# VectorE makes the first low part between the scalings of the second half, in the stage changes that have a shift

## The reference

```python
def modulate(h, shift, scale):
    return h * (1.0 + scale[:, None, :]) + shift[:, None, :]

sh, sc, g = mods[0], mods[1], mods[2]
h = modulate(rms_norm_2(x, norm_g[layer, 0]), sh, sc)
x = x + MACARON_WEIGHT * (1.0 + g)[:, None, :] * swiglu(h, ffn_w_in[layer, 0], ffn_w_out[layer, 0])
```

## Time and profile before

| what | value |
|---|---|
| device time, median of 3 runs | 1351.13 us (1350.64 to 1352.36) |
| the profiled execution, from first to last instruction (its span) | 1350.2 us |
| granted TensorE clock, mean | 0.998 of full |
| TensorE matmuls busy | 1317.2 us, 98% of the span |
| VectorE busy | 927.7 us, 69% |
| ScalarE busy | 661.8 us, 49% |

### The profile page before, as it was taken

How to read it: one execution, slowest core, us unless ns; L and a number is a source line. 1 busy time by engine, 2 the same in 40 slices (tenths; PEclk the granted TensorE clock), 3 DMA queues, 4 the chain that set the end, 5 groups by cost and what they waited for, 6 DMA issues and landing times.

```text
span 1350.2 us, 16397 instructions
## 1 busy us (share of the span) xinstructions
PE 1317.2 (98%) x6611; PEld 1084.1 (80%) x6611; DVE 927.7 (69%) x1023; ACT 661.8 (49%) x928; POOL 28.3 (2%) x56
## 2 busy tenths in 40 slices
PE   8998999999999999999999999999999999999998
PEld 8986677888887888888788888788888887788887
DVE  5368888766658776677866667966766786744444
ACT  5355765545446333335544335753333566644442
POOL 2200010000000000000000000000000000000000
PEclk9999999999999999999999999999999999999999
DMA  8996668777775777774678784588777632455551
GB/s 249 248 356 206 188 236 321 279 291 258 287 273 203 264 271 277 278 278 159 242 259 278 280 304 164 179 300 279 254 277 281 218 125 97 154 187 187 187 187 62
DMA packets 162762, 317.98 MB, mean 236 GB/s; under 512 B 7128, under 2 KB 108944, under 8 KB 153472
## 3 DMA queue, kind: packets, MB, share of 16 engines
q1 hardware_dynamic: 158800, 305.44, 65.8%
q0 software_dynamic: 3712, 11.45, 3.3%
q10 hardware_dynamic: 176, 0.05, 0.0%
HBM read 314.56 MB, written 1.84 MB: 234 GB/s over the span
## 4 chain that ended last, share of the span: by engine, by line
PE 85%; DVE 8%; ACT 3%; DMA 2%; issue 1%; SPq 0%; DVEq 0%; ACTq 0%
PE bank L735 26%; PE bank L737 26%; PE bank L736 26%; PE bank L833 2%; DVE full L1951 2%; DVE wlo L1855 1%; PE bank L756 1%; ACT whi L1376 1%; DMA raw<-in_cmp_w_v 1%; DMA ada<-in_ada_w 1%; DVE xt L1939 1%; DVE mix L1937 1%; PE bank L783 1%; DMA raw<-in_w_in 1%; PE bank L1091 0%
## 5 line engine op out<-in xcount | busy, mean ns | idle before, releaser
L1855 DVE TENSOR_TENSOR wlo<-raw,whi 128x2048 fp32r<-128x2048 f32 x202 | 462.6, 2291 | 231.7 <-ACT whi L1376 231.4
L1376 ACT ACTIVATE whi<-raw 128x2048 fp32r<-128x2048 f32 x205 | 392.2, 1914 | 190.1 <-PE bank L737 175.9
L735 PE MATMUL bank<-whi,uhi 128*128 128x512 f32 (+2 forms) x1168 | 454.1, 389 | 8.0 <-DVE ulo L1964 5.0
L737 PE MATMUL bank<-whi,ulo 128*128 128x512 f32 (+2 forms) x1168 | 445.7, 382 | 0.0
L736 PE MATMUL bank<-wlo,uhi 128*128 128x512 f32 (+2 forms) x1168 | 444.5, 381 | 0.0
L735 PEld LDWEIGHTS bank<-whi,uhi 128*128 128x128 f32 x1168 | 219.8, 188 | 54.2 <-issue 13.1
L737 PEld LDWEIGHTS bank<-whi,ulo 128*128 128x128 f32 x1168 | 219.6, 188 | 43.4
L736 PEld LDWEIGHTS bank<-wlo,uhi 128*128 128x128 f32 x1168 | 220.0, 188 | 40.6 <-issue 0.5
L735 PE MATMUL bank<-whi,hsplit 128*128 128x512 f32 (+1 forms) x512 | 200.9, 392 | 0.1
L737 PE MATMUL bank<-whi,hsplit 128*128 128x512 f32 (+1 forms) x512 | 198.5, 388 | 0.0
L736 PE MATMUL bank<-wlo,hsplit 128*128 128x512 f32 (+1 forms) x512 | 198.3, 387 | 0.0
(11 more groups left out here) (263 smaller groups left out, 951.2 us busy)
## 6 DMA issues: line engine op xcount, KB each, us to landing
raw<-in_ffn_w_in SPq DMA_DIRECT2D x176, 512.0 KB, 4.8
ada<-in_ada_w SPq DMA_DIRECT2D x72, 1024.0 KB, 7.3
raw<-in_ffn_w_out SPq DMA_DIRECT2D x44, 1024.0 KB, 5.0
raw<-in_w_in SPq DMA_DIRECT2D x16, 1024.0 KB, 9.1
raw<-in_w_mlp_in SPq DMA_DIRECT2D x16, 1024.0 KB, 6.8
raw<-in_w_mlp_out SPq DMA_DIRECT2D x16, 1024.0 KB, 5.0
ada<-in_kv_ada_w SPq DMA_DIRECT2D x8, 1024.0 KB, 7.2
raw<-in_w_kv SPq DMA_DIRECT2D x8, 1024.0 KB, 5.1
```

The costliest lines, as they stand in the source:

```text
L735: nc.tensor.matmul(o, sh, mh, start=start, stop=False, skip_group_check=skip)
L737: return nc.tensor.matmul(o, sl, mh, start=False, stop=stop, skip_group_check=skip)
L1376: ins = nc.scalar.activation(whi[:, ring(n), :], raw[:, ring(n), :], ACT.Copy)
L1855: ins = nc.vector.tensor_tensor(wlo[:, ring(n), :], raw[:, ring(n), :], whi[:, ring(n), :].bitcast(F32), ALU.subtract)
```

## The change

A new function `split_halves` does a whole pass on VectorE when there is a shift. The low part of the first half is no longer made after all eight scalings, but after six of them. The low part of the second half stays last. The same instructions are issued as before, with the same waits on their inputs. `turn` calls it for both passes of changes 2, 5, 6 and 7; change 1 keeps the old functions and order. The 4th change calls `make_full` and `u_low` itself and stays as it was. `conv(n + 1)` stands behind the pass of t = 0, as before. No queue but VectorE's has another order.

```diff
+            def split_halves(e, t, g, shift):
+
+                def low(c):
+                    dve.wait_ge(u_hi, 4 * e + 2 * t + c + 1)
+                    s = slice(4 * c, 4 * c + 4)
+                    nc.vector.tensor_tensor(ulo[:, s, t * P:(t + 1) * P], full[:, s, t * P:(t + 1) * P],
+                                            uhi[:, s, t * P:(t + 1) * P].bitcast(F32), ALU.subtract).then_inc(u_lo, 1)
+
+                def tile_of(c, k):
+                    kk = 4 * c + k
+                    return nc.vector.tensor_scalar(full[:, kk, t * P:(t + 1) * P], bank[2 * t + c][:, k * P:(k + 1) * P],
+                                                   g[:, kk:kk + 1], shift[:, kk:kk + 1], ALU.mult, ALU.add)
+
+                dve.wait_ge(u_turned, 4 * e + 2 * t + 1)
+                for k in range(3):
+                    tile_of(0, k)
+                tile_of(0, 3).then_inc(u_full, 1)
+                dve.wait_ge(u_turned, 4 * e + 2 * t + 2)
+                tile_of(1, 0)
+                tile_of(1, 1)
+                low(0)
+                tile_of(1, 2)
+                tile_of(1, 3).then_inc(u_full, 1)
+                low(1)
...
                 add_all(v)
                 if v == 6:
                     take_window(6, parts=(0,))
-                make_full(v, 0, g, shift)
-                u_low(v, 0)
-                if v != 2:
-                    conv(n + 1)
-                make_full(v, 1, g, shift)
-                u_low(v, 1)
+                for t in range(2):
+                    if shift is None:
+                        make_full(v, t, g, shift)
+                        u_low(v, t)
+                    else:
+                        split_halves(v, t, g, shift)
+                    if t == 0 and v != 2:
+                        conv(n + 1)
```

## The result

The changed kernel took 1355.51 us (median of 10 runs, 1353.27 to 1359.54), the kernel before 1351.38 us beside it (10 runs, 1350.64 to 1354.60). Two further comparisons on other chips, each with 12 runs of the changed kernel and 31 or 35 of the one before, gave 1.0015 (1.0005 to 1.0025) and 1.0021 (1.0013 to 1.0030), that is 1354.18 against 1352.38 us and 1355.07 against 1352.13. The mean of the three ratios is 1.0021, some 2.9 us. The forecast was +2.1 us and 1353.2 us, with a range to 1354.8: the direction and the places were right, two of the three medians lie outside the range, one (1354.18) inside.

What follows compares the result with a forecast made beforehand. TensorE, with 85% of the chain that ended last, was taken as the bound. Changes 7, 6, 2 and 5 gave 0.08 - 0.16 + 1.08 + 1.05, so 1351.1 + 2.1 = 1353.2 us, range 1350.7 to 1354.8.

Steps and rivals of the forecast that it cites:

- The pass: One VectorE pass, modelled on change 7: first low part 0.44 us earlier, everything behind it 0.81 us later.
- d: Delay of all that stands behind the moved low part on VectorE: 0.20 + 0.61 = 0.81 us.
- The gap in front of the first low part: VectorE stands for 0.20 us before the moved low part, until ScalarE's high part is finished.
- A handover of 0.03: Time from the end of ScalarE's high part to the start of VectorE's low part, 0.03 us.
- the strict reading: Next VectorE operation waits until the pipe is empty: low part holds the scaling 0.69 us, sum about +2.5 us.
- The norm behind the second high part: At t=0 ScalarE's norm for the second tokens comes late, so TensorE waits and the 0.44 us gain is lost.
- The four turns: TensorE's sums per change: change 7 +0.08, change 6 -0.16, change 2 +1.08, change 5 +1.05 us.
- Both tails: Work queued behind the pass in changes 2 and 5: TensorE's waits grow to near 2.3 and 1.3 us.
- What it loses stays lost: In these stages TensorE has no later wait for something that does not itself move, so lost time isn't recovered.
- slower by more than 0.2%: Rival: moved low part costs VectorE more at release and end; d from 0.91, 1354.1 us at 0.96; chance 0.25.
- Faster: Rival: TensorE keeps its earlier starts, tails covered and norm not late; at most 2.6 us, 1348.5; chance 0.07.
- Next to nothing: Rival: early starts come and later TensorE waits partly make good the tails; about 1351.1 us; chance 0.10.

Runs made afterwards that it cites:

- e8: Kernel before with two extra copies of 128x512 on VectorE in front of conv(b+2) in change 2: 1355.01 us, ratio 1.0017.
- e16: One profiled execution of the changed kernel with three extra VectorE copies ahead of conv(b+2) in change 2: 197.8 us from that wait to the next change, against 196.2.
- e15: Another profiled execution of the changed kernel with three extra VectorE copies ahead of conv(b+2) in change 2: 199.0 us from that wait to the next change, against 196.2.
- e6: Changed kernel with column sums moved between the passes in change 2 and conv(b+3) ahead of the sixteen scalings in change 5: 1350.37 us, ratio 0.9985.
- e2: Changed kernel with the new order only in change 5, the old one in changes 2, 6 and 7: 1353.04 us, ratio 1.0006.
- e11: Changed kernel with three extra copies of 128x512 on VectorE ahead of conv(b+2) in change 2, wait left empty: 1357.85 us, ratio 1.0036.

## Why the prediction was wrong

**The pass.** Right. The low part came 0.44 us earlier, the rest of the pass 0.81 later: d was taken as 0.81 and measured 0.81. The gap in front of the first low part was called 0.2 us; as VectorE's idle time it is 0.12, since the 0.2 counts from where a further scaling would start. A handover of 0.03 and a distance of 0.61 us held for the new sequence too (the two scalings start at 1158.29, 0.61 behind the low part). By the strict reading of the rule in the Trainium skill (VectorE: DVE Perf Modes, "The DRAIN you can't avoid") d would have been 0.89; the changed kernel's trace doesn't agree with that reading, with 0.61 us from a low part of 0.69 us to the scaling behind it.

**The norm behind the second high part.** Right: TensorE's new wait for L1413 was there in changes 2, 5 and 7 (0.47, 0.45 and 0.49 us), though not in change 6, and took the early start back. The products of (t 0, c 1) in change 7 came 7.46 us after the first scaling, where they had come at 7.00.

**The four turns.** At the places that it named, right within 0.04 us each, and the sum is 1.95 where 2.05 stood. Both tails grew as said: the waits were forecast near 2.3 and 1.3 and are 2.34 and 1.43. "What it loses stays lost" was nearly so: over whole stages the sum is 1.73 us, as TensorE won back 0.12 us in change 6 and 0.10 in change 7.

**The step that failed** is the one from this sum to the time: "so I predict 1351.1 + 2.1 = 1353.2 us". It took a longer wait to cost its own length, and put the cost beyond that at nothing without a reason. Measured are 2.9 us in the mean of three comparisons, against a path of 1.75 in the profiles: 1.2 us are left over (0.5 to 1.8, drawn again from the runs). What the runs showed in its place is that an empty wait can cost more than itself by way of TensorE's clock: 1.6 us behind a wait of 1.95 us (e8), 1.6 and 2.8 us behind one of 3.35 (e16, e15), and in the changed kernel a surcharge that sits in the executions with the lower mean clock and is gone when the waits are filled. That in the changed kernel too the clock falls behind the wait for slot b+2 is the likely reading and is not shown, since no trace of it has such a fall. The rival "slower by more than 0.2%" came out, but not by its mechanism: it asked for d of 0.91, and d was 0.81.

**The base.** The other part of the miss is the starting number. The median of 1351.13 us was from three runs; with 31 and 35 runs the kernel before has 1352.1 to 1352.4 on the later chips. The first comparison's 4.1 us between the medians are the largest of three (1.8 and 2.9 in the others), so part of that miss is chance; by the second alone the forecast would have stood. The forecast also set the profiled span of 1350.2 beside a median 0.9 us above it as if they belonged together. An execution's device time lies about 2.1 us above its own span (1353.27 and 1351.2 for the changed kernel), so the profiled execution took about 1352.3 us, near the highest of the three (1352.36). The forecast itself added to the median and did not suffer from it. Profiles of all kernels here reach change 1 between 227.2 and 232.5 us, so that single executions differ by up to 5 us ahead of anything that was changed. A range of 1 us above the slower rival was too narrow for that.

**The rivals.** *Faster* asked that the norm and the tails be off the path, and they were on it. Half of its chance was put beyond 2.7 us, though its own sum ends at 2.6. The Trainium skill (Perfetto Trace Analysis, "Optimizing Scalar/DVE Operations") says that breaking up instructions may allow work to be completed sooner; here no instruction was broken up, only the order changed, so no run tests the advice itself. The piece that was pulled forward did come 0.44 us earlier, and the time did not fall. e6 shows that even with both tails gone the new order is no faster than the old one. *Next to nothing* falls too: changes 2 and 5 cost 1.07 and 0.98 us over their whole stages.

Open stay how often the clock falls in the changed kernel, and whether the wait of 1.43 us in change 5 has a share in it. e2, with that wait alone, shows no surcharge, and none of the nine profiles with that wait empty has a fall there.

## What to carry to other kernels

An operation that is pulled forward on an in-order engine delays all that stands behind it, on its own engine and on the one that waits for its successor; follow both queues to the next place where the bounding engine waits, since here 0.44 us won at the front was paid with 0.81 at the back. When a change makes a wait of TensorE longer, add the chance of a fall of its clock to the price, and read the granted clock behind that wait in more than one execution. Single executions here differ by up to 5 us ahead of the place under study; the stretch from one fixed instruction to the next is the same within 0.1 us in every profile without a fall, so read the price of a change there. A wait found this way is itself the thing to change: moving two pieces of work out of the tails won about 2 us against the kernel before, in either order of the low parts.

## What the runs showed of the hardware that was not expected

In a kernel that keeps TensorE 98% busy, waits of 1.2 to 3.4 us were followed in some executions by a stretch of 3.4 us (in e15 of 6.8 us) at the lower of its two clocks, and in others of the same kernel by nothing. The stretch began while the wait lasted or up to 1.2 us behind its end. Length alone does not decide: the wait of 1.22 us at change 1 has a fall in 12 of 18 profiles, that of 2.07 us near 108 us in 7 of 18, that of 2.35 us in change 2 in none of 6, that of 3.35 us in 2 of 3 (e11's first profile has a granted clock of 1.00 behind it). Ahead of the wait of 1.22 us stand matmuls of 128x64, ahead of those in change 2 matmuls of 128x512; whether that makes the difference was not tested. Transposes of 128x128 of a constant in the wait cost nothing on the path, and with them the surcharge of the changed kernel was gone.
